# Low parts of most down weights: a negative high part from ScalarE, completed by an adding transfer on GpSimd's queue

## What is computed

```python
# first block, twice (ffn1, ffn2); D_FF = 2816
def swiglu(x, w_gu, w_down):
    g, u = jnp.split(x @ w_gu, 2, axis=-1)
    return (jax.nn.silu(g) * u) @ w_down
x = x + 0.5 * swiglu(rmsnorm(x, norm_ffn1_g), ffn1_w_gu, ffn1_w_down)
x = x + hybrid_mixer(...)            # projections, short convolution, gated linear attention
x = x + 0.5 * swiglu(rmsnorm(x, norm_ffn2_g), ffn2_w_gu, ffn2_w_down)
# second block; D_FF_2 = 4096
x = x + mix @ w_out                  # neighbourhood attention and retention
x = x + jnp.square(jax.nn.relu(rms_norm(x, norm_mlp) @ w_up)) @ w_down
```

## Time and profile before

| | before |
|---|---|
| median of 3 runs | 1753.71 us (1753.49 to 1754.31) |
| span of the profiled execution | 1751.3 us |
| TensorE busy | 1744.0 us, 10407 matmuls |
| VectorE busy | 1238.9 us |
| ScalarE busy | 850.4 us |
| GpSimd busy | 38.8 us |
| mean granted TensorE clock | 0.999 |

### The profile page before, as it was taken

One profiled execution on the slowest core, in us unless ns is written; L12 is line 12 of the kernel. 1 busy time (PEld: TensorE's weight loads), 2 busy tenths in 40 slices (PEclk: granted clock), 3 DMA queues, 4 the chain that ended last, 5 costly groups with the idle time before them and its releaser, 6 DMA issues.

```text
span 1751.3 us, 26596 instructions
## 1 busy us (share of the span) xinstructions
PE 1744.0 (100%) x10407; PEld 1534.4 (88%) x10407; DVE 1238.9 (71%) x1955; ACT 850.4 (49%) x1442; POOL 38.8 (2%) x38
## 2 busy tenths in 40 slices
PE   9999999999999999999999999999999999999998
PEld 7889989878888899988888998988877888989897
DVE  7949849666776557965795894976688677748474
ACT  6425526454333335743553562654655543627274
POOL 0000000000000000000000000000232000000000
PEclk9999999999999999999999999999999999999999
DMA  5232423332123232333323233334511233333232
GB/s 185 82 109 97 127 89 104 110 110 85 51 86 106 86 108 97 109 111 98 96 88 117 93 110 96 109 109 131 141 61 61 85 96 97 97 96 118 89 120 72
DMA packets 68427, 176.61 MB, mean 101 GB/s; under 512 B 8112, under 2 KB 9392, under 8 KB 68304
## 3 DMA queue, kind: packets, MB, share of 16 engines
q1 hardware_dynamic: 66576, 171.60, 31.4%
q10 hardware_dynamic: 1280, 2.08, 0.3%
q0 software_dynamic: 448, 1.24, 0.3%
HBM read 170.70 MB, written 2.10 MB: 99 GB/s over the span
## 4 chain that ended last, share of the span: by engine, by line
PE 95%; DVE 3%; ACT 1%; issue 1%; DMA 0%; DVEq 0%; ACTq 0%; POOLq 0%
PE ps L2064 18%; PE ps L2066 18%; PE ps L2065 18%; PE ps L2156 10%; PE ps L2158 10%; PE ps L2157 10%; PE ps L2086 2%; PE ps L2087 2%; PE ps L2088 2%; DVE wl L1159 1%; PE ps L2305 0%; ACT BThi L579 0%; PE ps L2435 0%; DVE BTlo L1231 0%; PE ps L2460 0%
## 5 line engine op out<-in xcount | busy, mean ns | idle before, releaser
L2064 PE MATMUL ps<-Ahi,wh 128*128 128x512 f32 x913 | 357.2, 391 | 0.0
L2065 PE MATMUL ps<-Alo,wh 128*128 128x512 f32 x913 | 355.4, 389 | 0.0
L2066 PE MATMUL ps<-Ahi,wl 128*128 128x512 f32 x913 | 355.4, 389 | 0.0
L2156 PE MATMUL ps<-BThi,wh 128*128 128x256 f32 x1232 | 340.6, 276 | 0.3 <-ACT tm L569 0.3
L2157 PE MATMUL ps<-BTlo,wh 128*128 128x256 f32 x1232 | 340.3, 276 | 0.0
L2158 PE MATMUL ps<-BThi,wl 128*128 128x256 f32 x1232 | 340.2, 276 | 0.0
L543 ACT ACTIVATE wh<-raw 128x1024 fp32r<-128x1024 f32 (+1 forms) x206 | 213.1, 1036 | 221.6 <-PE ps L2066 187.4
L1159 DVE TENSOR_TENSOR wl<-raw,wh 128x1024 fp32r<-128x1024 f32 (+1 forms) x206 | 250.1, 1215 | 64.6 <-ACT wh L543 62.6
L2156 PEld LDWEIGHTS ps<-BThi,wh 128*128 128x128 f32 x1232 | 231.3, 188 | 0.6 <-issue 0.6
L2157 PEld LDWEIGHTS ps<-BTlo,wh 128*128 128x128 f32 x1232 | 231.3, 188 | 0.0
L2158 PEld LDWEIGHTS ps<-BThi,wl 128*128 128x128 f32 x1232 | 231.3, 188 | 0.0
(11 more groups left out here) (355 smaller groups left out, 2707.7 us busy)
## 6 DMA issues: line engine op xcount, KB each, us to landing
raw<-in_w_gu SPq DMA_DIRECT2D x128, 256.0 KB, 2.8
raw<-in_w_d SPq DMA_DIRECT2D x32, 512.0 KB, 3.5
raw<-in_w_dn SPq DMA_DIRECT2D x32, 512.0 KB, 3.8
raw<-in_w_up SPq DMA_DIRECT2D x48, 256.0 KB, 2.8
raw<-in_w_gu SPq DMA_DIRECT2D x22, 512.0 KB, 3.6
raw<-in_w_d SPq DMA_DIRECT2D x16, 384.0 KB, 3.1
raw<-in_w_v SPq DMA_DIRECT2D x8, 512.0 KB, 3.8
raw<-in_w_cc SPq DMA_DIRECT2D x8, 512.0 KB, 3.6
```

Source lines behind the costliest of these rows:

```text
L2064: pe.matmul(ps, wh[:, c], hi[:, k, :], start=(k == 0), stop=False)
L2065: pe.matmul(ps, wh[:, c], lo[:, k, :], start=False, stop=False)
L2066: last = pe.matmul(ps, wl[:, c], hi[:, k, :], start=False, stop=(k == nb - 1))
L2156: pe.matmul(ps, whi[:, w], bhi, start=(new and kp == 0), stop=False, skip_group_check=not new)
```

## The change

It concerns the down units with n = 2 to 7 of every group, except the very last unit of the kernel: 59 units, 47 of 8 blocks and 12 of 6. For these (`DL`):
- ScalarE writes the high part as before, waits for it, and then writes minus the high part into the unit's `WL` buffer, as a second instruction (semaphore `neg`).
- VectorE makes no low part (`lo` returns at once).
- GpSimd waits for `neg` and issues a transfer that reads the same raw weights from HBM again and adds them to what stands in `WL` (`accum_op=ALU.add`). One semaphore for each of the three buffers (`far0`, `far2`, `far4`) counts the landings.
- TensorE waits at the unit's start for that landing and not for `wl`.
- SyncE waits for `neg` before it loads into a raw buffer whose last user was such a unit.

```diff
--- before.py
+++ after.py
@@ -80,6 +80,7 @@
 RN = []
 RF = []
 TZ = {}
+DL = {}
 
 
 def _units():
@@ -159,6 +160,8 @@
     bank_free, slot_free, raw_free, raw_count = {}, {}, {}, [0] * 6
     at = done = pe = w = ws = rs = 0
     last = None
+    far = 0
+    landed = [0] * 6
 
     def bank(banks):
         nonlocal at
@@ -174,12 +177,13 @@
         slot_free[i] = pe_done
         return i, free
 
-    def raw(wl_done, n):
+    def raw(done, n):
         nonlocal rs
         i = rs % 6
-        free = max(raw_free.get(i + j, 0) for j in range(n))
+        before = {raw_free[i + j] for j in range(n) if i + j in raw_free}
+        free = [(s, max(c for t, c in before if t == s)) for s in sorted({t for t, _ in before})]
         for j in range(n):
-            raw_free[i + j] = wl_done
+            raw_free[i + j] = done
         rs += n
         raw_count[i] += 16
         return i, raw_count[i], free
@@ -220,7 +224,7 @@
             WF.append([f for _, f in got])
             WN.append(wns)
             PEN.append(pens)
-            got = [raw(wns[c], 1) for c in (3, 3, 6, 4)]
+            got = [raw(("wl", wns[c]), 1) for c in (3, 3, 6, 4)]
             RSL.append([i for i, _, _ in got])
             RN.append([c for _, c, _ in got])
             RF.append([f for _, _, f in got])
@@ -248,12 +252,19 @@
             WN.append(0)
             RSL.append(2 * u)
             RN.append(0)
-            RF.append(0)
+            RF.append([])
             rs += 2
             continue
-        w += 1
-        WN.append(w)
-        i, c, free = raw(w, 2)
+        if name in ("w_d1", "w_d2", "w_dn") and n > 1 and u < len(plan) - 1:
+            far += 1
+            landed[i] += 16
+            DL[u] = far, landed[i]
+            WN.append(w)
+            i, c, free = raw(("neg", far), 2)
+        else:
+            w += 1
+            WN.append(w)
+            i, c, free = raw(("wl", w), 2)
         RSL.append(i)
         RN.append(c)
         RF.append(free)
@@ -277,7 +288,7 @@
 SEMS = [
     "raw0", "raw1", "raw2", "raw3", "raw4", "raw5", "sd", "tp", "tz", "bf", "bh", "bl", "fd0", "fd1", "fd2", "fd3", "x0", "x1", "x2", "x3", "x4", "x5", "x6", "x7", "vec", "ident",
     "mixc", "gd", "rope", "nam", "rb0", "rb1", "vb0", "vb1", "vb2", "vb3", "out",
-    "wh", "wl", "f0", "fh", "fl", "pe", "ev", "vo", "ao", "ones",
+    "wh", "wl", "neg", "far0", "far2", "far4", "f0", "fh", "fl", "pe", "ev", "vo", "ao", "ones",
     "hh", "hl", "sq", "ss", "ah", "al", "hn", "nh", "nl", "nsum", "nm", "na", "r", "tsum", "r4m", "r4s", "rt", "rrow", "rrow2",
     "silu",
     "vmm", "vt", "gp", "gz", "ga", "dd", "de", "qd", "kd", "ktr", "kstc", "sc", "std", "kv", "kvs", "oo", "od", "osq",
@@ -463,14 +474,15 @@
                 sp.wait_ge(s["fl"], 4)
             if u in PAIR:
                 for i, (row, half) in enumerate(((u + 1, 0), (u, 0), (u + 1, 1), (u, 1))):
-                    sp.wait_ge(s["wl"], RF[u][i])
+                    for done, count in RF[u][i]:
+                        sp.wait_ge(s[done], count)
                     sp.dma_start(RAWP[RSL[u][i]].rearrange("p (k n) -> p k n", k=4),
                                  src(row)[:, 4 * half:4 * half + 4, :]).then_inc(s[f"raw{RSL[u][i]}"], 16)
                 continue
             if u - 1 in PAIR:
                 continue
-            if RF[u] > 0:
-                sp.wait_ge(s["wl"], RF[u])
+            for done, count in RF[u]:
+                sp.wait_ge(s[done], count)
             k = UNITS[u][3] - UNITS[u][2]
             dst = RAW[RSL[u]][:, 0:128 * blocks(u)].rearrange("p (k n) -> p k n", k=k)
             sp.dma_start(dst, src(u)).then_inc(s[f"raw{RSL[u]}"], 16)
@@ -498,6 +510,14 @@
             for j in range(2):
                 pool.dma_start(RB[hp % 2][:, j, :], dr["rpb"][2 * hp + j]).then_inc(s[f"rb{hp % 2}"], 16)
 
+        def low(units):
+            for u in units:
+                k = UNITS[u][3] - UNITS[u][2]
+                pool.wait_ge(s["neg"], DL[u][0])
+                pool.dma_start(WL[WS[u]][:, 0:128 * k].rearrange("p (k n) -> p k n", k=k), src(u),
+                               accum_op=ALU.add).then_inc(s[f"far{WS[u]}"], 16)
+
+        low(u for u in DL if u < U0["nv"])
         pool.wait_ge(s["pe"], PEN[LAST2])
         raw_bias(0)
         raw_bias(1)
@@ -529,6 +549,7 @@
             if p % 4 == 2 and hp < 2:
                 pool.wait_ge(s["ng"], p + 2)
                 raw_bias(hp + 2)
+        low(u for u in DL if u > U0["nv"])
 
     def act_program(act):
         own = Own(act, s["ao"])
@@ -540,6 +561,12 @@
             act.wait_ge(s[f"raw{RSL[u]}"], RN[u])
             if WF[u] > 0:
                 act.wait_ge(s["pe"], WF[u])
+            if u in DL:
+                own.add(act.activation(WH[WS[u]][:, 0:n], RAW[RSL[u]][:, 0:n], ACT.Copy))
+                own.wait()
+                act.activation(WL[WS[u]][:, 0:n], f32(WH[WS[u]][:, 0:n]), ACT.Copy,
+                               scale=-1.0).then_inc(s["neg"], 1)
+                return
             act.activation(WH[WS[u]][:, 0:n], RAW[RSL[u]][:, 0:n], ACT.Copy).then_inc(s["wh"], 1)
 
         def pair_hi(p, c):
@@ -1145,7 +1172,7 @@
         own = Own(dve, s["vo"])
 
         def lo(u):
-            if u >= NU:
+            if u >= NU or u in DL:
                 return
             if u == U0["glr"]:
                 dve.wait_ge(s[f"raw{RSL[u]}"], RN[u])
@@ -2046,7 +2073,10 @@
             halves = u + 1 in PAIR and layer(u) != 1
             nb = blocks(u)
             ps, wh, wl = BK[BANK[u]][:, :], WH[WS[u]], WL[WS[u]]
-            pe.wait_ge(s["wl"], WN[u])
+            if u in DL:
+                pe.wait_ge(s[f"far{WS[u]}"], DL[u][1])
+            else:
+                pe.wait_ge(s["wl"], WN[u])
             if FREE[u] is not None:
                 pe.wait_ge(s[FREE[u][0]], FREE[u][1])
             for k in range(nb):
```

## The result

The changed kernel takes 1787.95 us (median of 4 runs, 1785.92 to 1790.87) where the kernel before takes 1754.01 us (4 runs, 1753.49 to 1755.24). The ratio is 1.0197, with a 95% interval of 1.0185 to 1.021: slower by 34 us, or about 2%. The prediction had the direction, and the time lies in its wide range, but it had a quarter of the size (7.8 us), and the time lies outside the likeliest case's own range of 1757 to 1770 us.

A forecast was written before the change was run, and what follows sets the result against it. TensorE's own work was taken to bound the kernel; stalls of 1.7 + 3.0 us (ffn's last groups), 2.7 (mlp) and 0.4 (first groups), 7.8 in all, gave 1761.5 us, 0.4% slower; range 1753.0 to 1804 us.

The forecast's parts named there:

- What bounds the kernel: Whole kernel: TensorE's own work sets the time, busy 1744.0 of 1751.3 us, with 2.5 us of waits.
- VectorE's 69 us: Down units: 59 subtractions leave VectorE, some 69 us of busy time, worth nothing because nobody waits for them.
- ScalarE's 60 us: Down units: 59 added negatives, 60 us of ScalarE's busy time, covered by its idle time and costing nothing.
- The chain up to the issue: Each 8-block unit: from the high part's start to GpSimd's issue 2.19 us; 1.74 us for 6 blocks.
- The rooms: Time left per unit for issue to landing: 8.4 us in most groups, down to 3.7 in ffn2's last.
- How long L is: L, the adding transfer's time from issue to landing: 5.2 us for 384 KB, 6.4 us for 512 KB.
- The term for what is in flight beside the transfer: Part of L for the raw load sharing the DMA engines: 0.45 us for 384 KB, 0.8 for 512 KB.
- the upper end: Highest landing times, with the raw load's full price: 5.8 us for 384 KB, 7.0 for 512 KB; 1769.7 us.
- The formula for the sum: Per group: landing minus room, counted once per stalling unit, n = 3 and 6 or 2 and 5; together 7.8 us.
- The addition is slow: Rival: each added byte costs four times a plain one, landings 7.3 and 9.2 us, 1801 us; chance 0.25.
- Hidden: Rival: landings near 3.4 to 3.7 us, below every room, so no cost, 1753.7 us; chance 0.26, including stalls under 3.5 us.
- TensorE gains: Rival: in ffn2's last group, removing VectorE's subtraction lets the next stage start sooner, at most 0.5 us, 1753.2 us; chance 0.02.

The follow-up runs named there:

- the 35 roomy units: The changed kernel with the adding transfer only for n = 3 to 7 of groups of 8 blocks, without mlp's last: 1756.08 us, ratio 1.0014.
- The plain transfer: The changed kernel with GpSimd's transfer writing the raw weights into the low part instead of adding them: 1759.62 us, ratio 1.0035.
- the raw loads late: The changed kernel with SyncE reloading a raw buffer only after GpSimd's transfer has landed: adding 1772.35 us, ratio 1.0109; writing without adding 1759.16 us, 1.0032.
- the half-size run: The changed kernel with the transfer adding only the first half of each unit's blocks, 256 KB or 192 KB: 1761.69 us, ratio 1.0049.

## Why the prediction was right and wrong

- *What bounds the kernel; VectorE's 69 us are worth nothing.* Right. VectorE did 66.7 us less, and without the transfer the time is the old one (1754.03 us).
- *ScalarE's 60 us are covered, and so is `neg` on SyncE's queue.* Right, by the same run.
- *The chain up to the issue: 2.19 us.* Nearly. GpSimd starts 0.30 us after the negative's end (101.01 to 101.31), where 0.05 was taken. Each room was a quarter of a microsecond too large.
- *The rooms and where it stalls.* Right in kind. Where room was given as 8.4 us the transfers of up to 8.4 us are hidden, but for some 2 us (the 35 roomy units), and the short rooms stall. Not all at the units foreseen: in the last groups it is n = 2, 4, 6 and 7 in ffn1 and n = 2, 3, 5 and 6 in ffn2, where n = 3 and 6 were named. The plain transfer, with 4.9 to 5.1 us, stalls in the last groups of `ffn` and nowhere else, as the rooms say. The stalls in the changed kernel are 4.8 us in ffn1's last group and 6.0 in ffn2's (predicted 1.7 and 3.0), 9.0 us in `mlp` (2.7) and 5.6 in the others (0.4).
- *How long L is.* This step failed: 6.4 us taken, 7.8 to 8.0 measured (384 KB: 5.2 and 6.4). The plain transfer was well sized (4.2 us taken, 3.7 to 4.2 measured with the raw loads late), and so was the second read in `ffn` (1.4 taken, 1.6 to 1.7 measured); in `mlp` it was 2.3. The term for what is in flight beside the transfer was not: 0.8 us taken; measured some 2.3 in the median in `ffn` (7.8 less 5.5), 1.5 in `mlp` (8.0 less 6.5), and 3.2 in the first two transfers; for 384 KB 0.45 taken and some 1.4 measured (6.4 less 5.0). Two things in it were wrong. The term held one raw load and put the neighbouring adding transfer at nothing; where n = 2 starts shortly ahead of n = 3, taking it away takes 1.0 us off the median landing of n = 3, and 3.1 us in ffn1's first group. And the argument was that the raw load is ahead by 0.6 us and so mostly through; the upper end let it be in the way with its full 1.4 us. Both ends treated the meeting as a displacement, and for the plain transfer that holds (0.8 to 1.3 us). For an adding one even the 1.9 us for which a raw load occupies the engines fall short of the 2.2 in `ffn`. So the upper end of 7.0 us was no bound.
- *The formula for the sum* holds in total. With the measured medians, 7.9 and 6.4 us, the same rooms give 4.1 + 5.4 us in the last groups of `ffn`, 3.4 + 2.0 in their first and second (rooms 6.2 and 6.9), and 1.4 + 2.4 + 2.4 + 3.7 in `mlp` (rooms of 6.5, 5.5, 5.5, and 5.5 and 6.6): 24.8 us where the trace has 25.4. With rooms shorter by 0.25 us it would be some 3 us more, so it is good to that much; since the units that stall are partly others, the closeness is in part luck.
- *Not in the sum:* the clock. Three stalls of over 2 us cost another 4.7 us of half speed, 3.9 us went in small delays around the stalls, and 2.2 us outside the groups. The prediction took a stall to cost its own length.
- *The rivals.* "The addition is slow" gave L of 7.3 and 9.2 us and 1801 us. Its time was nearer than the forecast's, and its price per byte is about what the half-size run shows, but its mechanism is not: with the raw loads late or absent the adding transfer for n = 2 takes 5.5 us in `ffn` and 6.2 to 6.7 in `mlp`, where a byte at four times the price would make it 8.4 (2.8 + 5.6). "Hidden" and "TensorE gains" fell.

The Trainium skill's Collectives: The Full Stack (The bandwidth ceiling), cited for an addition's costing two source reads and not more, agrees with the engine time of a transfer, 2.8 us against 1.5, and roughly with the landing where the raw loads are late: 5.5 us against 3.9 in `ffn`, 6.5 against 4.2 in `mlp`. It doesn't give the landing beside other loads, 8.7 us against 5.1 in the first two; there the measurement decides. The Trainium skill's DMA: Bandwidth & Descriptors (Issuing engines are not separate DMA queues), that transfers of all queues share the 16 engines, agrees: delaying SyncE's loads alone took 3.2 us off GpSimd's first two.

*Still open:* why an adding transfer suffers more from a neighbour than a plain one (its longer hold on engines that are nearly full would go with it, but some landings are as long with the engines at 69%); why it takes longer in `mlp` than in `ffn`; why the clock fell after some stalls of about 2 us and not after others; and why the halves in one unit set the pace of the pairs behind it. Adding into a buffer declared as plain float32 was not tried.

## What to carry to other kernels

Before moving work from an engine that has time to a chain with a deadline, work out each unit's room from the timeline, and then take a transfer's landing from a row in which it has the neighbours that it will have in the new place: sums of prices measured alone are no upper bound. A loss behind such a wait can be taken back by letting the waiting engine do first what does not need the operand (30 of 34 us here), but that only brings the kernel back to where it was, since the freed engine was not the bound. And where an edit changes how the last instructions of a unit are cut, compare the distance between instructions in the stretches that it doesn't touch.

## What was unexpected of the hardware

- An adding transfer of 512 KB lands in 5.3 to 5.7 us in `ffn` with the raw loads late, in 6.2 to 6.7 us in `mlp` with none beside its start, in 6.0 to 9.1 us with raw loads beside it; a plain one in 3.7 to 4.2 us (n = 2) and in 4.6 to 6.3 us.
- Issuing it holds GpSimd for 0.85 to 0.91 us.
- Matmuls of 256 columns ran 0.1133 or 0.1178 us apart over whole stretches of 76 us at full granted clock, depending on whether one unit ahead of them ended in two halves: 15 us in the kernel.
- A stall of TensorE of 2.3 to 2.8 us went, in three of four cases, with 1.4 to 1.6 us of loss at half the clock; in other runs the clock fell after 1.83 and 1.85 us of idle time and not after 2.35.
